# Stick-breaking scores: each head's four products alternate between the two halves of the partitions, with queries and keys copied by DMA with halves exchanged

## The reference, cut to what matters

```
z = jnp.einsum('bthd,bshd->bhts', q[:, t0:t1], kb) * scale       # per block of 128 queries
before = s_idx < t_idx
log_beta = jax.nn.log_sigmoid(z)
log_1m_beta = jnp.where(before, jax.nn.log_sigmoid(-z), 0.0)
tail = lax.cumsum(log_1m_beta, axis=3, reverse=True) - log_1m_beta
a = jnp.where(before, jnp.exp(log_beta + tail), 0.0)
out = jnp.einsum('bhts,bshd->bthd', a, vb)
```

## Time and profile before

| What | us |
|---|---|
| Median of 3 runs | 3476.04 (3475.92 to 3477.89) |
| The profiled execution, its own time | 3474.79 |
| Its span, first to last instruction | 3473.0 |
| PE busy in the span | 3157.7 (91%) |
| DVE, ACT, POOL busy | 2112.3, 1042.3, 1913.9 |
| First and last product of the stick-breaking scores | 977.5 and 1068.9 |
| Mean granted TensorE clock | 0.984 |

### The profile page before, as it was taken

How to read it: one execution, slowest core, us unless ns; L and a number is a source line. 1 busy time by engine, 2 the same in 40 slices (tenths; PEclk the granted TensorE clock), 3 DMA queues, 4 the chain that set the end, 5 groups by cost and what they waited for, 6 DMA issues and landing times.

```text
span 3473.0 us, 35165 instructions
## 1 busy us (share of the span) xinstructions
PE 3157.7 (91%) x12398; PEld 2119.0 (61%) x12398; DVE 2112.3 (61%) x3740; ACT 1042.3 (30%) x2538; POOL 1913.9 (55%) x1198
## 2 busy tenths in 40 slices
PE   7999999999999999999999999999988777777776
PEld 5778878887766788868777667544433333333332
DVE  5766543335764433369646776777666676667654
ACT  4562341112155211120132432333324332233222
POOL 4544259996502799968867555444444443444432
PEclk9999999999999999999999999999999999999999
DMA  4430022222321222323423124999999999999997
GB/s 163 169 134 1 1 85 97 97 97 85 133 85 37 87 97 96 114 73 122 141 72 112 38 88 153 399 421 417 418 421 416 421 422 421 421 421 422 421 419 303
DMA packets 108995, 741.70 MB, mean 214 GB/s; under 512 B 11816, under 2 KB 12968, under 8 KB 20776
## 3 DMA queue, kind: packets, MB, share of 16 engines
q0 software_dynamic: 73728, 536.90, 37.3%
q1 hardware_dynamic: 31488, 196.25, 16.1%
q10 hardware_dynamic: 3624, 6.56, 0.5%
HBM read 731.28 MB, written 8.39 MB: 213 GB/s over the span
## 4 chain that ended last, share of the span: by engine, by line
PE 64%; DMA 20%; DVE 8%; ACT 4%; issue 2%; POOL 2%; another core or an unknown queue 0%; DVEq 0%; POOLq 0%; ACTq 0%
DMA arena<-in_peer_uv,rstd 14%; PE bank L1285 13%; PE bank L1287 13%; PE bank L1286 13%; PE bank L1786 8%; DMA weight_ring<-in_peer_uv,rstd 3%; DMA normed<-in_peer_uv,rstd 3%; DVE arena L3216 2%; PE bank L1801 2%; PE bank L1716 1%; PE bank L1698 1%; PE bank L1584 1%; PE bank L1460 1%; PE bank L1477 1%; PE bank L1204 1%
## 5 line engine op out<-in xcount | busy, mean ns | idle before, releaser
L1142 POOL DMA_INDIRECT arena<-in_peer_uv,rstd x419 | 454.2, 1084 | 635.7 <-PE bank L1786 590.9
L3216 DVE CUSTOM_DVE_ANT_0 arena<-arena,branch 128x1024 f32<-128x1024 f32 x419 | 510.7, 1225 | 336.6 <-DMA arena<-in_peer_uv,rstd 331.1
L1287 PE MATMUL bank<-split_arena 128*128 128x512 f32 x1776 | 696.6, 392 | 0.0
L1055 POOL TENSOR_TENSOR split_arena<-weight_ring,ones 128x1024 fp32r<-128x1024 f32 x204 | 506.3, 2482 | 151.3 <-PE bank L1287 97.6
L1285 PE MATMUL bank<-split_arena 128*128 128x512 f32 x1392 | 545.9, 392 | 5.3 <-DVE split_normed L2644 2.5
L1286 PE MATMUL bank<-split_arena 128*128 128x512 f32 x1392 | 541.7, 389 | 0.0
L1057 POOL TENSOR_TENSOR split_arena<-weight_ring,split_arena 128x1024 fp32r<-128x1024 f32 x204 | 519.3, 2546 | 16.0
L1786 PE MATMUL bank<-arena,row_diagonals 128*128 128x512 f32 x836 | 402.4, 625 | 91.5 <-ACT row_diagonals L2372 91.1
L1786 PE MATMUL bank<-arena,level_mask 128*128 128x512 f32 x840 | 390.1, 606 | 76.7 <-ACT level_mask L2372 76.7
L1287 PEld LDWEIGHTS bank<-split_arena 128*128 128x128 f32 x1776 | 334.0, 188 | 72.5
L1786 PEld LDWEIGHTS bank<-arena,row_diagonals 128*128 128x128 f32 x836 | 159.8, 198 | 315.8 <-issue 171.2
(11 more groups left out here) (475 smaller groups left out, 4965.5 us busy)
## 6 DMA issues: line engine op xcount, KB each, us to landing
weight_ring<-in_w_up SPq DMA_DIRECT2D x32, 1024.0 KB, 4.8
weight_ring<-in_w_down SPq DMA_DIRECT2D x32, 1024.0 KB, 4.8
weight_ring<-in_w_in SPq DMA_DIRECT2D x32, 1024.0 KB, 5.0
weight_ring<-in_ada_w SPq DMA_DIRECT2D x24, 1024.0 KB, 5.0
weight_ring<-in_w_in_a SPq DMA_DIRECT2D x12, 1024.0 KB, 6.8
weight_ring<-in_w_out SPq DMA_DIRECT2D x12, 1024.0 KB, 7.0
weight_ring<-in_w_in_b SPq DMA_DIRECT2D x10, 1024.0 KB, 6.9
arena<-in_peer_uv,rstd POOLq DMA_INDIRECT x419
```

What stands on the lines that cost most here:

```text
L1055: pool.tensor_tensor(hi, part, bc_mid(ones[:], DT), ALU.mult).then_inc(split_hi, 1)
L1142: pool.indirect_dma_start(row_slots[slot_of[r]], None, a["peer_uv"], bass.IndirectOffsetOnAxis(ap=experts[n % 2][:, c:c + 1], axis=0)).the ...
L1287: return pe.matmul(psum[t.bank][:], hi, a_lo[k], start=False, stop=last)
L3216: dve.tensor_tensor_reduce(row, row, h_tok[:, r // NE, :], 1.0, 0.0, ALU.mult, ALU.add, dots[:, i % 4, j:j + 1]).then_inc(dot_ready, 1)
```

## The change

`stick_scores` takes the products in the order 0, 1, 2, 3 and alternates between the halves: product `j` of head `h` reads partitions of half `(h + j) % 2`. Products 0 and 2 use the head's own half of `sq_f` and `sk_f`. Products 1 and 3 use copies `sq_x` and `sk_x`, in which the two halves of the partitions are exchanged. SyncE makes these copies by DMA inside SBUF, four DMAs of 64 partitions by 2 KB (128 KB) for each of the six tiles. The copies of tiles 0 and 1 go to four tiles that are free by then; the copies of tiles 2 to 5 overwrite tiles 0 to 3 of `sq_f` and `sk_f`, once their heads' products are done. The order of the tail sums stays 0, 1, 3, 2. In the changed kernel the line of the products is L1598, and other lines are 3 to 29 higher.

```
         STICK_ORDER = (0, 1, 3, 2)
 
-        def score_tiles(h):
-
-            t = {j: aux(3 * (h % 2) + (0, 1, 2, 1)[j]) for j in STICK_ORDER}
+        def score_tiles(h, order=STICK_ORDER):
+
+            t = {j: aux(3 * (h % 2) + (0, 1, 2, 1)[j]) for j in order}
             return [t[j] for j in range(TT)]
 
-        stick.append({"z": score_tiles(0)})
+        stick.append({"z": score_tiles(0, range(TT))})
         for h in range(SH + 1):
             if h + 1 < SH:
-                stick.append({"z": score_tiles(h + 1)})
+                stick.append({"z": score_tiles(h + 1, range(TT))})
...
+        first_x = region(M_HID + (2 * QT + DT + 1) * SEQ, 4)
+        sq_x, sk_x = [[first_x[:, i, :], first_x[:, 2 + i, :]] + [x[:, p, :] for p in range(MT - 2)] for i, x in enumerate((sq_f, sk_f))]
...
+        rows_swapped = [sem(f"stick_rows_swapped{i}") for i in range(2)]
...
-            for u in units[mlps[0]["first"] + 8 * QUARTERS:mlps[1]["first"]]:
+            for u in units[mlps[0]["first"] + 8 * QUARTERS:out_units[1][0].u]:
+                load(u)
+
+            def swap_rows(p):
+
+                if p < 2:
+                    sp.wait_ge(half_done, 2 * (sq_units[-1].u + 1))
+                    for i in (p, MT + p):
+                        have(sp, sq_tiles[i])
+                else:
+                    full(sp, stick[2 * p - 3]["z"][TT - 1])
+                for src, dst in ((sq_f, sq_x), (sk_f, sk_x)):
+                    for a, b in ((0, SD), (SD, 0)):
+                        sp.dma_start(dst[p][b:b + SD], src[a:a + SD, p, :]).then_inc(rows_swapped[p % 2], 16)
+
+            for p in range(2):
+                swap_rows(p)
+            for u in out_units[1]:
+                load(u)
+            for p in range(2, MT):
+                swap_rows(p)
+            for u in units[out_units[1][-1].u + 1:mlps[1]["first"]]:
                 load(u)
...
             def stick_scores(h):
-                r = slice((h % 2) * SD, (h % 2) * SD + SD)
-                for j in STICK_ORDER:
+                if h % 2 == 0:
+                    pe.wait_ge(rows_swapped[h // 2 % 2], 64 * (h // 4 + 1))
+                tile = h // 2
+                for j in range(TT):
                     t = stick[h]["z"][j]
                     if j < TT - 1:
                         free(pe, t)
-                    pe.matmul(stick_score(t, j), blk(sk_f[r, h // 2, :], j), sq_f[r, h // 2, j * P:], start=j < TT - 1,
+                    half = (h + j) % 2
+                    r = slice(half * SD, half * SD + SD)
+                    keys, queries = (sk_x[tile], sq_x[tile]) if j % 2 else (sk_f[:, tile, :], sq_f[:, tile, :])
+                    pe.matmul(stick_score(t, j), blk(keys[r, :], j), queries[r, j * P:], start=j < TT - 1,
                               stop=True, skip_group_check=True).then_inc(psum_full, 1)
```

## The result

| | us |
|---|---|
| Changed kernel, median of 20 runs | 3483.12 (3481.66 to 3484.97) |
| Kernel before beside it, median of 20 runs | 3476.82 (3475.47 to 3479.18) |
| Ratio, 95% interval | 1.0017 (1.0012 to 1.0023), +6.3 us |
| Profiled execution, span after and before | 3481.3 and 3473.0 |

A forecast was written before the change was run, and what follows sets the result against it. The prediction took a chain through TensorE, ScalarE and VectorE to bound the scores stage. Its terms, +4.1 wait, +1.7 clock, -0.85 head 0, -2.1 pairs and tail, sum to +2.85: 3478.9 us, range 3475.0 to 3484.5.

The forecast's parts named there:

- Wait for the copies: Ahead of head 0's products, TensorE waits for tile 0's copies queued behind the last modulation weight's load: +4.1 us.
- Clock behind it: After TensorE's wait at head 0, the clock falls to half pace for 3.4 us in dense products: +1.7 us.
- Head 0's block at full clock: Head 0's score block, on TensorE's own path, shortens from 2.35 to 1.50 us as halves overlap: -0.85 us.
- Pairs and tail: In the scores stage, five pairs of heads and the tail each gain 0.35 us on the chain: -2.1 us.
- rival 2: Score products: the halves do not run together, so the order costs +0.45 six times; total +8.5, 3484.5 us; chance 0.11.
- the 1.2 us for the copies: In SyncE's queue, tile 0's 0.5 MB lands 1.2 us behind the load, at the loads' 2.47 us per MB.
- rival 1: Tile 0's copies move at half the rate: 2.47 us for 0.5 MB, wait 5.3, total +4.1, 3480.1 us; chance 0.22.
- Rivals 3 and 4: Tile 0's copies: 3, one after another, wait 13.2, 3488, chance 0.07; 4, pass the load, wait 2.3, 3477.1, chance 0.13.
- the second block's 0.85: In a pair's second score block, TensorE's 0.85 us saving is off the path because VectorE's result comes later.
- Passes of the halves: Sign in the score blocks: passes of the two halves start within 0.02 us of each other, block of 1.5 us.
- Copies of later tiles: The later sixteen copies are hidden; a wait for a later tile's copy would show the prediction wrong.
- Rival 5: Scores stage: TensorE's whole gain comes through, 1.7 us a pair; -3.55 with wait and clock, 3472.5 us; chance 0.05.

The follow-up runs named there:

- e1: Changed kernel with the first eight copies issued earlier, ahead of the load of the last value unit: 3473.91 us, ratio 0.999 to the kernel before.
- e5: Changed kernel with tile 0's four copies issued directly ahead of the last modulation weight's load instead of behind it: 3474.18 us, ratio 1.0001 to the kernel before.
- e6: Changed kernel with two full-width copies of 128 partitions per tile, halves not exchanged (scores not the reference's): 3477.83 us, ratio 1.0013 to the kernel before.
- e8: Changed kernel with the first eight copies read from memory instead of SBUF (heads 0 to 3 not the reference's): 3481.05 us, ratio 1.0013.
- e9: Changed kernel with tiles 0 and 1 copied together in four DMAs of 4 KB rows, all awaited (scores of heads 0 to 3 wrong): 3486.43 us, ratio 1.0025.
- e11: Changed kernel with SyncE issuing nothing more until tile 0's four copies have landed: 3483.2 us, ratio 1.002 to the kernel before.
- e4: Changed kernel with seven unread products of 512 columns keeping TensorE busy ahead of its wait for the first copies: 3480.39 us, ratio 1.0008.
- e7: As e1, with VectorE's four diagonal masks per head cut to one column (scores not the reference's): 3469.0 us, ratio 0.9989 to the kernel before.
- e3: As e1 with early copies, but every product reads its head's own half, in order 0, 1, 2, 3: 3481.58 us, ratio 1.0014 to the kernel before.
- e10: As e1, with VectorE's four diagonal masks of a head merged into one instruction: 3473.78 us, ratio 0.9988 to the kernel before.

## Why the prediction was right or wrong

**Right in the places, short in the sizes.** The shape of the forecast held: a wait at head 0 with a DMA as its releaser, a fall of the clock with it, halves of rows that run together, a gain in each pair far below what TensorE saves. In numbers:

| Step | forecast | measured |
|---|---|---|
| Wait for the copies | +4.1 | +6.3 (6.3 to 7.0) |
| Clock behind it | +1.7 | +3.2 |
| Head 0's block at full clock | -0.85 | -0.87 (1.48 in e1) |
| Pairs and tail | -2.1 | -2.6 |
| Sum | +2.85 | +6.0; by the medians +6.3 |

That the time still lies in the range is partly luck. Its upper end, 3484.5, was set by rival 2, whose mechanism did not come; no case inside the range had both halves that overlap and a wait of over 5.3 us.

**The wait (4.1).** The step that failed is the 1.2 us for the copies: that they move behind the load at its 2.47 us for each MB, and that the load still lands after 4.9. The load ahead took 1.5 us longer (6.4), and the fourth copy landed 1.7 behind it: 8.15 in place of 6.1. Another 0.2 us passes between the last landing and the first product (the "issue" of 0.24 in e5's chain), which the sum left out. Four causes were tried by themselves, and none carries the difference: the half width (e6, wait 5.90), the source in SBUF (e8, 6.06), the short rows (e9, 10.1 for twice the bytes), what stands behind (e11, 6.28). Each was changed alone, so two of them together are not ruled out, and no run gave the copies a queue of their own beside the load. Shown is that it takes the load ahead: without it the same copies land in 2.3 (e5, and the second four of e11). Shown is also that load and copies together move less in a microsecond than loads alone. Why they hinder each other in one queue stays open. Of rival 1's mechanism (5.3, half rate) e6 leaves 0.3 to 1.1 us of its 1.2 in this wait; it shows more plainly in the bytes behind. Rivals 3 and 4 are out: the copies did not run one after another, and the fourth did not pass the load.

**The clock (1.7).** The step took the 3.4 us of low clock of an earlier, shorter wait as a fixed length. Here 0.50 was reached 3.7 us ahead of the wait's end and held until 6.5 us behind it. What it cost is read from one start to the next: head 0's block 2.82 us instead of 1.48, and the value unit 15.73 (989.04 to 1004.77) instead of 13.92 (e1, 977.66 to 991.58), 1.34 + 1.81 = 3.2. e4 gives 3.2 of it back in its rows at an unchanged wait, and 2.9 in the medians, so this term is shown, not only argued.

**The pairs (2.1).** The step took 0.35 for each of six stretches, and was short in both halves of a pair.

- The first block: the `Exp` comes 0.46 earlier behind it (2.44 against 2.90). The step had found 0.32 "or a little more". Of that 0.44 is left at the second block, which starts 5.98 behind the first (1041.07 to 1047.05) instead of 6.42 (1045.72 to 1052.14).
- The second block brings another 0.17, which the step left out. Before, the sums' first product started at 1054.49, 2.35 behind that block's start, when the block ended; VectorE's L2810 had ended at 1054.26, 2.12 behind the earlier trace rows. Now the block itself takes 1.88 (e7) and the sums begin at 2.18, as soon as VectorE is done (1048.62 + 0.56).

The prediction wrote that the second block's 0.85 was not on the path because VectorE came later. VectorE came later than the shortened block, but 0.2 earlier than the end of the old one. Its own numbers say so: L2810's end less 0.35 is 1053.91, and from 1054.49 that is over 0.5, not 0.35. Nor does TensorE save 0.85 there; it saves 0.47, since the second block waits for banks.

So a regular pair gains 0.61 (14.72 to 14.11). But there are three of these (1026.96 to 1069.30 is three times 14.11). The two heads ahead of them take 14.37 (-0.35, 1012.59 to 1026.96), the way from head 1's block to head 2's 6.53 (+0.08), and from 1069.30 to the next stage's first product (L1309, 1092.83) it is 23.53 instead of 24.05. Together -1.83 - 0.35 + 0.08 - 0.52 = -2.6. The same from the whole: that product is 8.34 later than in the kernel before (1084.49), of which 2.3 were there at the entry, and 6.3 + 3.2 - 0.87 = 8.6 came ahead of the stage; 8.3 - 2.3 - 8.6 = -2.6.

**What would have shown it wrong.** Passes of the halves were to start within 0.02 us of each other; they start 0.10 apart (1041.51 and 1041.61), which the block's length of 1.49 does not mind. Copies of later tiles were never waited for; the only wait for a copy in the stage is the first. Rival 5 (pairs at 13 us) is out by the 14.11, and rival 2 by the 1.49. Rival 2's price for the order alone, +0.45 in a pair's first block, was near: e3 measured +0.38 a pair.

**The better version.** e1 is ahead of both kernels: 3.1 us under the kernel before (interval 0.3 to 6.6, so only just clear of it), 9.4 under the changed one. e10 is the same time.

## What to carry to other kernels

A transfer that an engine will wait for costs what stands ahead of it in its queue, so ask first whether its source was ready earlier: here the copies' place was worth 9.4 us, three times the whole gain of the new products. Price TensorE's wait as two terms, the wait and the slow clock that goes on after it; the second was half of the first. When an engine is made faster inside a chain of three, take the gain from each hand-over (who ends last, and by how much the next one is behind it), not from busy time: of 1.3 us that TensorE saved in a pair of blocks, 0.61 came through, 0.17 of it because the block had ended 0.2 us behind the engine that was taken for the later one.

## What the runs showed of the hardware that was not expected

- A copy of 64 or 128 partitions by 2 KB takes SyncE about 0.6 us to issue (mostly 0.52 to 0.73), from SBUF or from memory. A load of 128 partitions by 8 KB takes 0.33 to 0.43 behind other loads, but 0.58 to 0.60 directly behind copies of 64 partitions (e5, e8, e11, the changed kernel).
- Such copies land in 2.2 to 2.4 us with nothing ahead of them in the queue, and those directly behind a load of 1 MB in 5.1 to 6.8; the load then takes 6.0 to 7.1 instead of 4.9.
- With 64 partitions on either side the copies move at a lower rate than with 128: 240 to 309 GB/s (changed kernel) against 410 to 449 (e6) in windows of 1 us behind the load, and 12.0 us against 9.2 for load and 1 MB of copies (e9, e6). The wait for the first 0.5 MB shows little of it.
- In six of the fourteen profiled executions the granted clock fell once more to 0.50 inside the stage or on the way into it: e1 (at 1001.3), e3 (996.8), e4 (1072.9), e5 (1007.8), e8 (1060.0) and e9 (1064.5). Each lost at most 1.7 us by it. TensorE had small waits ahead of most of them, but so it had in the other executions; e3 has it with the long blocks, and what decides whether it comes stays open. e1's two heads there took 15.2 us (999.40 to 1014.62), the changed kernel's 14.4. In its profile e1 comes to the next stage 2.6 us earlier than before, counted from the products with `ones`; without this 0.85 it would be -0.87 - 2.6 = -3.5. It takes back part of what the pairs gain.
